# Time mixing on one core: the gate projection's slices stand behind 12 of the 18 stages of a body instead of behind all 18

## What is computed

```python
P = h @ w_in
P_rw, P_sa, P_ret, P_gate = split_cols(P, (RW_COLS, SA_COLS, RET_COLS, GATE_COLS))
y_rw, s_rw_new, shift_new = rwkv_mixer(P_rw, shift_rw, s_rw, lp)
...
def step(S, inp):                          # in rwkv_mixer, token after token
    r_t, w_t, k_t, v_t, kk_t, a_t = inp
    removed = jnp.einsum('bhvk,bhk->bhv', S, kk_t)
    S = (S * w_t[:, :, None, :]
         - removed[..., None] * (kk_t * a_t)[:, :, None, :]
         + v_t[..., None] * k_t[:, :, None, :])
    return S, jnp.einsum('bhvk,bhk->bhv', S, r_t)
...
gates = jax.nn.sigmoid(P_gate.astype(F32)).astype(x.dtype).reshape(B, L, N_BRANCH, D_MODEL)
merged = (gates[:, :, 0] * (y_rw @ lp['w_br_rwkv']) + gates[:, :, 1] * ... + gates[:, :, 2] * ...)
```

## Time and profile before

| | us |
|---|---|
| three runs | 2712.65, 2706.03, 2711.05 |
| median | 2711.05 |
| the profiled execution | 2707.16 |
| its span in the profile | 2705.4 |
| PE busy in it | 2592.2 |
| bodies 1 to 3 of layer 1 (588.8 to 739.9) | 151.1 |
| bodies 1 to 3 of layer 2 (1926.8 to 2078.1) | 151.3 |

### The profile page before, as it was taken

One profiled execution on the slowest core, in us unless ns is written; L12 is line 12 of the kernel. 1 busy time (PEld: TensorE's weight loads), 2 busy tenths in 40 slices (PEclk: granted clock), 3 DMA queues, 4 the chain that ended last, 5 costly groups with the idle time before them and its releaser, 6 DMA issues.

```text
span 2705.4 us, 61384 instructions
## 1 busy us (share of the span) xinstructions
PE 2592.2 (96%) x24742; PEld 2396.8 (89%) x24742; DVE 1313.2 (49%) x2242; ACT 563.8 (21%) x1117; POOL 1058.7 (39%) x596
## 2 busy tenths in 40 slices
PE   8997999999999999999999979998999899999998
PEld 7996887799879999999989868877998699999998
DVE  5357886544545621121543588756444555211215
ACT  2022222411123210011210222223111322110112
POOL 4522333221124555565544324322111255555553
PEclk9998999999999999999999989999999999999999
DMA  5212112211134322222232111122111352222221
GB/s 191 87 42 72 54 58 69 103 51 46 45 120 155 99 79 86 86 78 85 86 132 71 60 52 58 55 77 108 44 39 39 133 170 87 79 86 84 79 85 66
DMA packets 66730, 222.81 MB, mean 82 GB/s; under 512 B 8256, under 2 KB 9024, under 8 KB 65472
## 3 DMA queue, kind: packets, MB, share of 16 engines
q1 hardware_dynamic: 45360, 160.59, 17.5%
q10 hardware_dynamic: 21136, 58.84, 6.3%
HBM read 190.38 MB, written 29.03 MB: 81 GB/s over the span
## 4 chain that ended last, share of the span: by engine, by line
PE 82%; DVE 9%; DVEq 5%; issue 2%; ACT 1%; DMA 0%; ACTq 0%
PE dense L523 67%; PE mix L523 14%; DVEq L1542 5%; DVE region_b L1801 1%; DVE region_b L1902 1%; PE mix L954 0%; DVE region_b L1913 0%; DVE x L1854 0%; ACT region_b L1072 0%; DVE region_b L1578 0%; DVE region_b L1973 0%; DVE act_lo L1560 0%; PE dense L954 0%; DVE region_b L1889 0%; DVE region_b L2007 0%
## 5 line engine op out<-in xcount | busy, mean ns | idle before, releaser
L507 POOL TENSOR_SCALAR w_hi<-w_raw 128x1024 fp32r<-128x1024 f32 x296 | 311.1, 1051 | 1599.6 <-PE dense L523 1237.5
L510 POOL TENSOR_TENSOR w_lo<-w_raw,w_hi 128x1024 fp32r<-128x1024 f32 x296 | 747.5, 2525 | 24.7
L523 PE MATMUL dense<-act_hi,w_hi 128*128 128x288 f32 x2272 | 692.7, 316 | 29.0 <-DVE act_lo L1560 13.4
L523 PE MATMUL dense<-in_hi,w_hi 128*128 128x288 f32 x2432 | 678.6, 294 | 11.4 <-DVE in_lo L2031 8.7
L523 PE MATMUL dense<-in_lo,w_hi 128*128 128x288 f32 x2432 | 678.3, 295 | 0.0
L523 PE MATMUL dense<-act_lo,w_hi 128*128 128x288 f32 x2272 | 651.6, 298 | 0.0
L523 PE MATMUL dense<-act_hi,w_lo 128*128 128x288 f32 x2272 | 535.5, 297 | 0.0
L523 PE MATMUL dense<-in_hi,w_lo 128*128 128x288 f32 x2432 | 522.0, 296 | 0.0
L523 PEld LDWEIGHTS dense<-act_hi,w_hi 128*128 128x128 f32 x2272 | 433.3, 191 | 89.3 <-issue 44.6
L523 PEld LDWEIGHTS dense<-in_hi,w_hi 128*128 128x128 f32 x2432 | 458.6, 189 | 13.4 <-DVE in_lo L2031 8.9
L523 PEld LDWEIGHTS dense<-in_lo,w_hi 128*128 128x128 f32 x2432 | 458.9, 189 | 0.0
(11 more groups left out here) (200 smaller groups left out, 2657.9 us busy)
## 6 DMA issues: line engine op xcount, KB each, us to landing
w_raw<-in_stream SPq DMA_DIRECT2D x296, 512.0 KB, 3.2
y_mix<-gate_scratch ACTq DMA_DIRECT2D x48, 288.0 KB, 2.9
gate_scratch<-region_b ACTq DMA_DIRECT2D x36, 288.0 KB, 2.1
x_scratch<-x ACTq DMA_DIRECT2D x2, 2304.0 KB, 13.1
y_scratch<-y_mix ACTq DMA_DIRECT2D x2, 2304.0 KB, 7.8
x<-x_scratch ACTq DMA_DIRECT2D x2, 2304.0 KB, 11.9
y_mix<-y_scratch ACTq DMA_DIRECT2D x2, 2304.0 KB, 9.1
gate_scratch<-region_a ACTq DMA_DIRECT2D x12, 288.0 KB, 2.1
```

What stands on the lines that cost most here:

```text
L507: nc.gpsimd.tensor_scalar(w_hi[:, v, :], w_raw[:, s, :], 1.0, 1.0, ALU.mult, ALU.mult).then_inc(w_high, 1)
L510: nc.gpsimd.tensor_tensor(w_lo[:, v, :], w_raw[:, s, :], w_hi[:, v, :].bitcast(F32), ALU.subtract).then_inc(w_split, 1)
L523: return nc.tensor.matmul(out, lhsT, rhs, start=start, stop=stop, skip_group_check=True)
```

## The change

One weight for all stages of a body becomes one weight for each stage. In bodies 1 to 4, gram, turn, m0, m1, x1 and m2 have weight 0 and the other twelve stages weight 3 in place of 2; bodies 0 and 5 stay as they are.

```diff
-BODY_SHARE = (3, 2, 2, 2, 2, 2)
+BODY_SHARE = ((3,) * 12,) + ((0, 3, 0, 3, 0, 3, 3, 0, 3, 0, 3, 0, 3, 3, 3, 3, 3, 3),) * 4 + ((2,) * 3,)
+assert all(len(w) == n for w, n in zip(BODY_SHARE, BODY_STAGES))
...
-    first, shares = sum(MID_FILL), [n * w for n, w in zip(BODY_STAGES, BODY_SHARE)]
+    first, shares = sum(MID_FILL), [sum(w) for w in BODY_SHARE]
     total = (N_GATE - GATES_DSA) * KT - first
-    at = sum(shares[:body]) + stage * BODY_SHARE[body]
-    return first + at * total // sum(shares), first + (at + BODY_SHARE[body]) * total // sum(shares)
+    at = sum(shares[:body]) + sum(BODY_SHARE[body][:stage])
+    return first + at * total // sum(shares), first + (at + BODY_SHARE[body][stage]) * total // sum(shares)
```

## The result

| | before | after |
|---|---|---|
| median | 2706.03 us (five runs, 2698.18 to 2712.65) | 2687.05 us (five runs, 2682.74 to 2687.35) |
| ratio | | 0.9924, 95% interval 0.9906 to 0.9941 |
| profiled execution, its span | 2707.16, 2705.4 | 2687.32, 2685.5 |

The kernel is faster by 0.76%, 19.9 us between the two spans. With two more runs the median of before fell from 2711.05 to 2706.03; the ratio applied to that gives 2685.5, which is just under the low end of 2686.0. So the direction and the main mechanism came out as forecast, and the gain was put too small.

The account below looks back on a forecast made before the run. The prediction took TensorE's own stream to bound the kernel. Its terms, 16.3 + 4.2 + 1.5 + 0.3 - 2.3 - 2.0 = 18.0 us, off the three-run median 2711.05 gave 2693.0 us, range 2686 to 2704.5.

Parts of the forecast that it names:

- Fewer passages: Bodies 1 to 4, both layers: 48 fewer runs of fill between small blocks, at 0.34 us each, save 16.3 us.
- rival 1: Only the fill's half of each passage is saved, 8.2 us in place of 16.3; time 2701.1 us, chance 0.15.
- rival 3: The passage cost stays whole, belonging to the stage and its wait; only 1.7 us gained, 2709.3 us, chance 0.12.
- The wait at body 4: Body 4's gram stops waiting 2.09 us for VectorE, as POOL's split no longer delays the preparation; 4.2 us saved.
- Rival 2: The wait at body 4's start stays under another cause, the clock too: 5.7 us less gain, 2698.7 us, chance 0.15.
- The clock behind it: Layer 2, behind body 4's wait: the granted clock no longer falls to 0.51, saving 1.5 us more.
- The waits that come: New waits at m0 for ACT's copies and at turn for VectorE's mask, costing 2.3 us together.
- Gaps for code: Longer runs of small blocks outrun their instructions: two more gaps of about 0.5 us a layer, 2.0 us lost.
- Rival 4: Slower: moved splits land on VectorE's two-operand work before a stage needing it; with twelve, 2724.0 us; chance 0.06.
- The collision that the prediction saw in body 1: Body 1, split behind m3: the preparation of group 2 loses some 0.6 us but is done two us before gram.

Follow-up runs that it names:

- before again: The kernel before, unchanged, profiled once more in a single execution: 2710.33 us.
- shifted: The kernel before with one slice of body 1 moved from stage 12 to stage 17: 2701.68 us in one execution.
- later_gram: The kernel before with two slices moved from body 2 to the end of body 1: 2709.55 us in one execution.
- split_back: The changed kernel with the end of body 3 as before, so the tile ends behind x3 again: 2696.22 us, ratio 0.9947 to before.
- tail_bare: The changed kernel's 12 fills a body, but the six stages without fill are the last six of bodies 1 to 4: 2716.60 us, ratio 1.0032 to before.
- nine_tuned: The changed kernel with only nine fills in bodies 1 to 4, and slices rearranged in bodies 0 and 2: 2681.22 us, ratio 0.9907 to before.
- moved_split: The kernel before with one slice of body 3 moved from stage 7 to stage 17: 2704.84 us, ratio 0.9984 to before.

## Where the prediction held, and the step that failed

- **Fewer passages: right.** 16.3 predicted, 16.1 found (0.19 of the 0.335 with the slices, where the prediction read 0.16 to 0.18). The step that rested on thin evidence, that a chain's own fixed part goes as well and not only the fill's, held: rival 1 is out (gram and r show it directly), and rival 3 with it. The reading of x2's inner distances, with a satisfied wait between them that cost nothing, was what told.
- **The wait at body 4: right, for the reason given**, shown from both sides, by moving one slice of the kernel before and by putting the changed kernel's end of body 3 back. Rival 2 falls. One number in that step was wrong: I wrote that one slice stands behind x3 in body 3, and there are two, so that the slot comes free 3.9 us after x3 and not 3.0. It made the cover longer and changed nothing.
- **The clock behind it: right in this pair, by luck.** The drop to half clock (1.2 GHz) behind the wait is not there every time: it followed six of the ten such waits in before, before again, shifted, later_gram and split_back, in one layer or the other or both; of waits of the same size elsewhere it followed both of 2.2 us in tail_bare and neither of 2.13 us in nine_tuned. The prediction took the one layer of the one execution that it had.
- **The waits that come: right** to 0.1 us in sum. m0 stands 0.47 us in bodies 1 and 3 alike. The 0.2 more that I added in body 3 for the split on VectorE's work behind gram did not show: the split did hold an operation there (2.84 us), but m0 waited for ACT. The sum is that close because this 0.4 too much met 0.4 too little at m0 and 0.1 at turn.
- **Gaps for code: the step that failed.** I took the one gap of 0.34 shown in gram as a thing that longer runs must multiply, and put it at -2.0 us between 0 and -4. The gap that was there went, with 0.55 in both layers and another 0.26, so that the term was +1.4: 3.4 us off, and nearly all of the 3.5 us by which the gain in the bodies (21.5) was put too small (18.0). What the runs showed in place of "longer runs outrun their instructions" is that the gaps stand at one position of each block of 256 instructions, whatever the length of the run: the changed kernel has runs of 160 matmuls and no gap, and in moved_split, shifted and later_gram a u stage of 16 matmuls between two fills has one, of 0.27 to 0.82 us between starts. Why no block comes late in its order stays open. I gave the term no side above nothing, though the change moves nearly every instruction of the bodies in the code and can as well take a gap away. With a bound of +1.5 the low end of the range, 2686.0 with no gaps, would have been 2684.5.
- **The base.** The sum was taken from a median of three runs that lay 5 us above that of five. The ratio, 0.9924 against a forecast of 0.9934, is off by 0.10 points. Of the 7.5 us between 2693.0 and 2685.5, 5.0 are this base and 2.6 the gain.
- **Rival 4** did not occur in the changed kernel, and it did in nine_tuned at 2.13 us a layer. Both times that a split held TensorE, in before and there, it lay on the preparation behind x3. The collision that the prediction saw in body 1 came as it said: a copy of the preparation (L1625) took 0.76 us instead of 0.17, and gram did not wait.

## What to carry to other kernels

When a bound engine alternates between two kinds of work, measure the fixed cost of the alternation from distances between starts, not from busy time, and put filler only where the next stage waits for something fresh; everywhere else let the independent chains cover each other. Then check for each moved piece of filler what its end releases on the other engines: one slice of six matmuls moved a weight split onto or off a VectorE operation, worth more than six junctions. A stall that depends on where code falls can go as well as come, so its term needs a bound on both sides of nothing.

## What the hardware showed that I had not expected

- Passing from 64x64 f32 blocks to 128x288 slices and back costs 0.335 us (0.19 with the slices, 0.15 with the blocks), none of it idle in the profile; passing between blocks of different operands, PSUM banks and semaphores that are already there costs nothing that can be seen (gram to r at 0.029 us a matmul).
- A VectorE operation with two SBUF operands is held by POOL's split: 2.58, 2.69 and 2.85 us instead of 0.42 to 0.69, while operations with one operand in PSUM keep their 0.42. In the bodies of all thirteen profiled executions 88 of VectorE's tensor_tensor operations with both operands in SBUF began while POOL was making a low part, and all took longer than outside a split; of 427 with one operand in PSUM none did.
- Stages of the same program repeat to 0.01 us from layer to layer and from execution to execution (228.93 and 228.95 us for bodies 0 to 5, twice), while the whole program spreads over 0.2 to 0.5%. A change of 1 us in a stretch can be read in the profile long before it can be timed.
